# A hybrid decoder layer: the tokens' gate table moved from GpSimd to VectorE, and one transposed token tile copied out a weight piece earlier

## The chip, the cores and the metric

One NeuronCore of one Trainium2 chip. The engines are TensorE (PE in the profile, with its weight loads as PEld), VectorE (DVE), ScalarE (ACT), GpSimd (POOL) and SyncE (SP), which only issues transfers here. The metric is device time in microseconds (us). The time of the kernel before is 1771.23 us, the median of three runs from 1770.09 to 1771.25 us.

## What is computed

The reference is one layer on 512 tokens of 1024 channels: a mixer (gated delta rule and RG-LRU), a cross attention over 256 memory tokens, and a mixture of experts, then a last RMSNorm. The change touches the experts' part only:

```python
logits = xt @ w_router + b_router                 # 512 x 32
top_logit, top_e = lax.top_k(logits, TOP_K)       # 4 of 32 experts for each token
gate = jax.nn.softmax(top_logit, axis=-1)
...
gt = jnp.minimum(xblk @ w_gate[e] + b_gate[e], SWIGLU_LIMIT)
up = jnp.clip(xblk @ w_up[e] + b_up[e], -SWIGLU_LIMIT, SWIGLU_LIMIT)
hid = (up + 1.0) * (gt * jax.nn.sigmoid(SWIGLU_ALPHA * gt))
return hid @ w_down[e] + b_down[e]
...
y = yb.reshape(n_rows, D) * row_gate[:, None]
out = jax.ops.segment_sum(y, row_tok, num_segments=n_tok + 1)[:n_tok]
```

The tokens' rows are sorted by expert into blocks of 128 rows of one expert (`xblk`), and the blocks' results are summed up by token.

## The kernel before

All weights are float32. Each 128x1024 piece of a weight matrix is split in two parts: ScalarE writes the high part (`hi`, L1003 in the experts, L713 before them), VectorE subtracts it from the weights and writes the low part (`lo`, L1888 in the experts, L1616 before them), and TensorE multiplies three products of parts. In the experts a matrix has 8 pieces, a block of 128 rows needs 24 (gate 0 to 7, up 8 to 15, down 16 to 23), and there are 6 buffers of split pieces, so that ScalarE writes piece c when TensorE has used piece c-6. The 4 MB matrices lie in a ring of three; SyncE starts the load that reuses a place when VectorE has written the last low part out of it.

The order of the work is written out by hand on each engine, with semaphores between them. Each of the engines runs its list in order, so whatever stands behind a waiting instruction waits too.

**Around the router.** The last projection of the attention is done in 16 pieces, c = 0 to 15. TensorE's order is: piece 9, transposes of token tile 0, piece 10, transposes of tile 1, pieces 11 and 12, router products of tile 0 (L1411; they wait until the four copies of tiles 0 and 1 are out, `tr_evac`), piece 13, router of tile 1 and half the transposes of tiles 2 and 3, piece 14, halves of their router products, piece 15, the rest. VectorE at step c writes the low part of piece c+2, adds the residual at c = 7 and c = 11 (L1812), and copies the transposes out with `evac_h2` (L1883). ScalarE writes the high part of piece c+2 when TensorE has used piece c.

**Before and in the loop of the experts.** TensorE, VectorE and ScalarE do the first block as soon as the tables stand. POOL's list at that point is, with its lines: gather the rows of the second block (L583), build the gate table (L602 to L614), clear `gate_sb`, wait until the gates lie in DRAM (`gate_out`), two additions that make row numbers (`take`, L591), gather the rows' gates (L595), and then in the loop fetch the bias rows of the next block (L629), gather the rows of the block after it, and scatter the block's result. ScalarE waits for the gates of the rows before it scales a block's result (L1071); TensorE waits for the bias rows (`bias4_in`) before the first matmul of a block (L1496).

The gate table `g_parts` holds, for each token and each of 32 experts, the token's gate or zero, split in three parts. It is read once, in the last of the 32 blocks: TensorE transposes it (L1526, after `iota_ready` has reached 2), ScalarE copies it out (L1061), and the products with the experts' output biases (L1561) start the sum of the last rows. VectorE's list in a block (`expert_lo`) is: low parts 6 to 12, the product with the sigmoid (L2045), low parts 13 to 18, clipping and product of the two halves of the hidden rows (L2056, L2058, each twice), the low parts of the hidden rows (L2061) with pieces 19 to 21 between, then `x_lo` and pieces 22 and 23. After each half of the hidden rows TensorE transposes it (L1533) and goes on to the down matrix (L1546). The low parts 0 to 5 of the next block stand at the end of the loop's body.

Of the kernel before, what the change touches and what calls it, by code (L numbers as in the profile page):

```python
# [20 lines left out]
ALU = mybir.AluOpType  # L21
ACT = mybir.ActivationFunctionType
AX_X = mybir.AxisListType.X
F32 = mybir.dt.float32
BF16 = mybir.dt.bfloat16
F32R = mybir.dt.float32r
# [3 lines left out]
P = 128  # L30
# [4 lines left out]
def build_layer(nc, x, mem, norm_mix, w_in, dn_conv, dn_a_log, dn_dt_bias, dn_norm, rg_conv, rg_conv_b,  # L35
# [33 lines left out]
    with ExitStack() as ctx:  # L69
# [64 lines left out]
        def split_w(c, part):  # L134

            i = c % NSPLIT
            return wsp[:, (i + 2) % 4, part] if i < 4 else wsp_b[:, 5 - i, part]
# [216 lines left out]
        nf_row, bd_rows, bd_parts = ring[:, GM, 0, :], ring[:, GM, 1, :], split_w(0, 0)  # L354
        g_parts, g_stack = extra[:, 4, 0:NT * 3 * E].rearrange("p (t c) -> p t c", t=NT), bias4[0:3 * E, T:2 * T]
# [87 lines left out]
        def _(pool):  # L443
            chain = [0]

            def link(ins):
                chain[0] += 1
                ins.then_inc(pool_c, 1)
                pool.wait_ge(pool_c, chain[0])
# [97 lines left out]
            e_row = extra[:, 4, 384:384 + E]  # L547
# [54 lines left out]
            pool.wait_ge(codes_ready, 2)  # L602
            top_e = extra[:, 5, 128:160].rearrange("p (t k) -> p t k", t=NT)
            one = extra[:, 5, 256:512].rearrange("p (t k e) -> p t k e", t=2, k=TOPK)
            for t in range(0, NT, 2):
                for u in range(2):
                    for k in range(TOPK):
                        last = pool.tensor_scalar(one[:, u, k], e_row, top_e[:, t + u, k:k + 1], gates[:, t + u, k:k + 1], ALU.is_equal, ALU.mult)  # L608
                link(last)
                link(pool.tensor_tensor(one[:, :, 0:2], one[:, :, 0:2], one[:, :, 2:4], ALU.add))  # L610
                link(pool.tensor_tensor(g_parts[:, t:t + 2, 2 * E:3 * E], one[:, :, 0], one[:, :, 1], ALU.add))
            for c in range(2):
                link(pool.tensor_copy(g_parts[:, :, E * c:E * (c + 1)].bitcast(F32R), g_parts[:, :, 2 * E:3 * E]))
            pool.tensor_tensor(g_parts[:, :, 2 * E:3 * E], g_parts[:, :, 2 * E:3 * E], g_parts[:, :, 0:E], ALU.subtract).then_inc(iota_ready, 1)  # L614
# [970 lines left out]
        def _(dve):  # L1585
# [341 lines left out]
            for c in range(N_CO):  # L1927
# [11 lines left out]
                if c == 11:  # L1939
                    evac_h2(1, 0, 6, 3)  # L1940
                    evac_h2(1, 1, 7, 4)
# [96 lines left out]

            def expert_lo(n, last=False):
# [37 lines left out]

            expert_lo(n_more, last=True)
# [51 lines left out]
```

## Time and profile before

| what | value |
|---|---|
| median of three runs | 1771.23 us |
| the profiled execution's own time | 1772.93 us |
| its span in the trace | 1771.2 us |
| TensorE busy | 1690.2 us, 95% of the span |
| VectorE busy | 1437.0 us, 81% |
| ScalarE busy | 1274.6 us, 72% |
| GpSimd busy | 527.8 us, 30% |
| mean granted clock of TensorE | 0.987 of full speed |

The busy share of TensorE is so high that the view of busy times says little more than that time can be won only where TensorE stands still or runs at the lower of its two clock levels (1.2 instead of 2.4 GHz). The experts take the stretch from about 580 us to the end. The profile's queues and lines are read with the chain of waits (the work that ended last, followed back), the list of waits, and each engine's timeline; where a group of like instructions is merged, its duration runs from the first start to the last end. Starts are in us from the span's start.

### The profile page before, as it was taken

Reading aid. Unit: us, or ns where it says so; the run is one execution under the profiler, and the core shown is the slowest. Engines: PE = TensorE matmul, PEld = TensorE weight load, DVE = VectorE, ACT = ScalarE, POOL = GpSimd, SP = SyncE. Lnnn points to the kernel's source line nnn. Section 1 sums busy time; section 2 is a strip of 40 time slices with the busy share of each in tenths; the row PEclk is TensorE's granted clock in tenths of the full one; section 3 lists DMA queues with packets and bytes.
Section 4 is the critical chain, followed back from the end, with each engine's and each line's share of the span. In section 5 each row is a group of like instructions: output and inputs, shape, how many; then the busy total and the mean of one; then the engine's idle time right before and its main releaser. Section 6 shows DMA issues by size and latency. Waiting matters only on the chain.

```text
span 1771.2 us, 24520 instructions
## 1 busy us (share of the span) xinstructions
PE 1690.2 (95%) x8065; PEld 1385.7 (78%) x8065; DVE 1437.0 (81%) x1531; ACT 1274.6 (72%) x1452; POOL 527.8 (30%) x624
## 2 busy tenths in 40 slices
PE   6999799899899989999999999999999999999997
PEld 3778598787768768888888888888888888888885
DVE  3558686663347969999999999999999999999997
ACT  4453454464435668888888888888888888888885
POOL 3453552200022822242222222232232323232232
PEclk9999999999998989999999999999999999999999
DMA  7312100042014879999999999999999999999993
GB/s 249 119 51 100 41 1 1 24 190 95 26 82 191 330 271 369 360 383 378 355 371 371 382 359 370 360 382 379 351 371 369 379 364 369 360 380 379 353 371 120
DMA packets 53880, 476.18 MB, mean 269 GB/s; under 512 B 10503, under 2 KB 11640, under 8 KB 29266
## 3 DMA queue, kind: packets, MB, share of 16 engines
q1 hardware_dynamic: 42528, 450.70, 62.8%
q0 software_dynamic: 11120, 24.91, 6.3%
q8 instruction: 25, 0.41, 0.1%
q14 instruction: 13, 0.11, 0.0%
q10 hardware_dynamic: 194, 0.06, 0.0%
HBM read 461.24 MB, written 23.08 MB: 273 GB/s over the span
## 4 chain that ended last, share of the span: by engine, by line
PE 61%; DVE 18%; issue 12%; ACT 6%; POOL 3%; DMA 1%; ACTq 0%; POOLq 0%; DVEq 0%
PE ps L1546 20%; PE ps L1506 17%; PE ps L1143 10%; PE ps L1304 4%; DVE wsp L1888 4%; DVE extra L2058 2%; DVE extra L2056 2%; DVE wsp_b L1888 2%; ACT extra L1048 2%; POOL extra L608 1%; PE ps L1533 1%; PE ps L1227 1%; DVE wf L1616 1%; PE ps L1239 1%; PE ps L1496 1%
## 5 line engine op out<-in xcount | busy, mean ns | idle before, releaser
L1888 DVE TENSOR_TENSOR wsp<-ring,wsp 128x1024 fp32r<-128x1024 f32 x512 | 601.1, 1219 | 26.6 <-ACT wsp L1003 26.1
L1003 ACT ACTIVATE wsp<-ring 128x1024 fp32r<-128x1024 f32 x388 | 387.0, 1051 | 80.2 <-PE ps L1488 53.0
L580 POOL TENSOR_TENSOR guard<-guard 1x1 f32<-1x1 f32 x219 | 133.8, 616 | 763.0 <-ACT extra L1071 327.9
L1506 PE MATMUL ps<-wsp,x_hi 128*128 128x512 f32 x1152 | 311.8, 392 | 0.6 <-DVE x_lo L2014 0.6
L1888 DVE TENSOR_TENSOR wsp_b<-ring,wsp_b 128x1024 fp32r<-128x1024 f32 x256 | 301.8, 1218 | 9.8 <-ACT wsp_b L1081 9.1
L1506 PEld LDWEIGHTS ps<-wsp,x_hi 128*128 128x128 f32 x1152 | 217.5, 189 | 50.1 <-issue 1.1
L1003 ACT ACTIVATE wsp_b<-ring 128x1024 fp32r<-128x1024 f32 x194 | 205.5, 1060 | 32.3 <-PE ps L1506 11.0
L1506 PE MATMUL ps<-wsp,x_lo 128*128 128x512 f32 x576 | 179.1, 392 | 0.0
L1616 DVE TENSOR_TENSOR wf<-ring,wf 128x1024 fp32r<-128x1024 f32 x64 | 81.3, 1273 | 111.8 <-ACT wf L713 111.8
L713 ACT ACTIVATE wf<-ring 128x1024 fp32r<-128x1024 f32 x80 | 84.2, 1055 | 117.4 <-PE ps L1143 62.2
L1143 PE MATMUL ps<-act_hi,wf 128*128 128x512 f32 x512 | 161.6, 397 | 2.6 <-DVE wf L1616 2.1
L1081 ACT ACTIVATE wsp<-ring 128x1024 fp32r<-128x1024 f32 x124 | 131.9, 1064 | 36.8 <-PE ps L1546 36.8
L1546 PE MATMUL ps<-wsp_b,hid_hi 128*128 128x512 f32 x512 | 140.2, 395 | 0.0
L1506 PE MATMUL ps<-wsp_b,x_hi 128*128 128x512 f32 x512 | 136.8, 389 | 0.0
L1546 PE MATMUL ps<-wsp,hid_hi 128*128 128x512 f32 x512 | 136.8, 389 | 0.0
L1506 PEld LDWEIGHTS ps<-wsp,x_lo 128*128 128x128 f32 x576 | 108.6, 189 | 23.4
L1488 PE MATMUL ps<-wsp,x_hi 128*128 128x512 f32 x384 | 118.2, 389 | 0.0
L1143 PEld LDWEIGHTS ps<-act_hi,wf 128*128 128x128 f32 x512 | 95.7, 188 | 27.5 <-issue 8.1
L1546 PEld LDWEIGHTS ps<-wsp,hid_hi 128*128 128x128 f32 x512 | 96.1, 188 | 20.0
L1506 PEld LDWEIGHTS ps<-wsp_b,x_hi 128*128 128x128 f32 x512 | 96.1, 188 | 20.0
L1546 PEld LDWEIGHTS ps<-wsp_b,hid_hi 128*128 128x128 f32 x512 | 93.6, 188 | 22.8 <-issue 4.8
L1143 PE MATMUL ps<-act_lo,wf 128*128 128x512 f32 x256 | 99.8, 390 | 0.0
(380 smaller groups left out, 2993.9 us busy)
## 6 DMA issues: line engine op xcount, KB each, us to landing
ring<-in_w_gate_dram SPq DMA_DIRECT2D x32, 4096.0 KB, 15.3
ring<-in_w_up_dram SPq DMA_DIRECT2D x32, 4096.0 KB, 14.4
ring<-in_w_down_dram SPq DMA_DIRECT2D x32, 4096.0 KB
ring<-in_w_in_dram SPq DMA_DIRECT2D x6, 2048.0 KB, 12.0
ring<-in_w_ckv_dram SPq DMA_DIRECT2D x4, 2048.0 KB, 10.1
ring<-in_w_out_dram SPq DMA_DIRECT2D x2, 2048.0 KB, 10.6
ring<-in_w_cq_dram SPq DMA_DIRECT2D x2, 2048.0 KB, 11.1
ring<-in_w_co_dram SPq DMA_DIRECT2D x2, 2048.0 KB, 10.6
```

The lines of the kernel that those rows point to most:

```text
L580: return pool.tensor_tensor(guard[:, i:i + 1], guard[:, 0:1], guard[:, 0:1], ALU.mult)
L713: act.activation(parts_of(f, 0), piece(f), ACT.Copy).then_inc(wfh_ready, 1)
L1003: act.activation(split_w(c, 0), ring[:, m, k], ACT.Copy).then_inc(hi_ready, 1)
L1048: act.activation(gs, ps[:, 0:2, :].rearrange("p b f -> p (b f)"), ACT.Sigmoid, scale=1.702).then_inc(sg_ready, 1)
L1081: act.activation(split_w(c, 0), ring[:, GM, c], ACT.Copy).then_inc(hi_ready, 1)
L1143: last = pe.matmul(o, parts_of(f, w)[:, k], a[:, k], start=(k == 0 and w == 0 and a is a_hi), stop=(k == KT - 1 and a is a_lo))
L1304: last = pe.matmul(ps[:, banks[b]], a[:, rows + kk, ts], parts_of(f, w)[:, kk], start=(first and kk == 0 and a is a_hi and w == 0), stop=( ...
L1488: o = pe.matmul(ps[:, bank + i], xp[:, c % KT * P:(c % KT + 1) * P], split_w(c, w)[:, i * 512:(i + 1) * 512], start=False, stop=(last_k an ...
L1506: last = pe.matmul(ps[:, 2 * j + i], xp[:, k * P:(k + 1) * P], split_w(c, part)[:, i * 512:(i + 1) * 512], start=False, stop=(k == KT - 1 ...
L1546: last = pe.matmul(ps[:, 4 + i], xp[:, k * P:(k + 1) * P], split_w(c, part)[:, i * 512:(i + 1) * 512], start=(k == 0 and xp is hid_hi and ...
L1616: dve.tensor_tensor(parts_of(f, 1), piece(f), parts_of(f, 0), ALU.subtract).then_inc(wfl_ready, 1)
L1888: dve.tensor_tensor(split_w(c, 1), ring[:, (GM + c // KT) % 3, c % KT], split_w(c, 0), ALU.subtract).then_inc(lo_ready, 1)
```

## The change

Two edits. First, the gate table is built by VectorE at the start of the last block, ahead of its `expert_lo`, and no longer by POOL between its first gather and the clearing of `gate_sb`. On POOL one table took 16 products of 128x32, 4 additions, 2 copies and a subtraction; on VectorE it takes, for each pair of token tiles, two comparisons, two products and two reductions, each over 128x128, and after both pairs two copies and a subtraction, with a wait after each group. The definition of `e_row` moves up for this. Second, the two copies of token tile 1's transposes stand at c = 10 and not at c = 11.

```diff
--- before.py
+++ after.py
@@ -352,6 +352,7 @@
         LAST_BANKS = ((0, 1), (2, 3), (6, 7), (4, 5))
         last_tok, last_f, last_oh = extra[:, 5, :].bitcast(I32), extra[:, 5, :], bias4[:, 0:T]
         nf_row, bd_rows, bd_parts = ring[:, GM, 0, :], ring[:, GM, 1, :], split_w(0, 0)
+        e_row = extra[:, 4, 384:384 + E]
         g_parts, g_stack = extra[:, 4, 0:NT * 3 * E].rearrange("p (t c) -> p t c", t=NT), bias4[0:3 * E, T:2 * T]
         ylo_ready, YLO = yt_ready, 4
         sum_mm, SUM_MM = out_mm, 8
@@ -544,7 +545,6 @@
             link(pool.iota(it_i[:, 417:418], pattern=[[0, 1]], base=4 * T + 1, channel_multiplier=4))
             link(pool.tensor_copy(ef[:, 64:80], it_i[:, 64:80]))
             link(pool.tensor_copy(ef[:, 288:418], it_i[:, 288:418]))
-            e_row = extra[:, 4, 384:384 + E]
             link(pool.tensor_copy(ef[:, 0:E], it_i[:, 0:E]))
             link(pool.tensor_copy(e_row, it_i[:, 0:E]))
             link(pool.tensor_scalar(ef[:, 32:64], ef[:, 0:E], float(CAP * P), None, ALU.mult))
@@ -599,19 +599,6 @@
 
             link(take(0, tok_tab, slice(CAP, CAP + 1)))
             gather()
-            pool.wait_ge(codes_ready, 2)
-            top_e = extra[:, 5, 128:160].rearrange("p (t k) -> p t k", t=NT)
-            one = extra[:, 5, 256:512].rearrange("p (t k e) -> p t k e", t=2, k=TOPK)
-            for t in range(0, NT, 2):
-                for u in range(2):
-                    for k in range(TOPK):
-                        last = pool.tensor_scalar(one[:, u, k], e_row, top_e[:, t + u, k:k + 1], gates[:, t + u, k:k + 1], ALU.is_equal, ALU.mult)
-                link(last)
-                link(pool.tensor_tensor(one[:, :, 0:2], one[:, :, 0:2], one[:, :, 2:4], ALU.add))
-                link(pool.tensor_tensor(g_parts[:, t:t + 2, 2 * E:3 * E], one[:, :, 0], one[:, :, 1], ALU.add))
-            for c in range(2):
-                link(pool.tensor_copy(g_parts[:, :, E * c:E * (c + 1)].bitcast(F32R), g_parts[:, :, 2 * E:3 * E]))
-            pool.tensor_tensor(g_parts[:, :, 2 * E:3 * E], g_parts[:, :, 2 * E:3 * E], g_parts[:, :, 0:E], ALU.subtract).then_inc(iota_ready, 1)
             link(pool.memset(gate_sb[:], 0.0))
             pool.wait_ge(gate_out, 16)
             pool.wait_ge(acc_in, 16 * NT)
@@ -1936,7 +1923,7 @@
                 if c == 9:
                     evac_h2(0, 0, 4, 1)
                     evac_h2(0, 1, 5, 2)
-                if c == 11:
+                if c == 10:
                     evac_h2(1, 0, 6, 3)
                     evac_h2(1, 1, 7, 4)
                 if c == 13:
@@ -2036,6 +2023,25 @@
             dve.wait_ge(codes_ready, 1)
             n_more = dve.value_load(nblocks[0:1, 1:2], min_val=E - 1, max_val=MAXB - 4)
 
+            def gate_table():
+
+                one = extra[:, 5, 256:512].rearrange("p (t k e) -> p t k e", t=2, k=TOPK)
+                for t in range(0, NT, 2):
+                    for u in range(2):
+                        ins = dve.tensor_tensor(one[:, u], e_row.unsqueeze(1).to_broadcast([P, TOPK, E]),
+                                                tf4[:, t + u].unsqueeze(2).to_broadcast([P, TOPK, E]), ALU.is_equal)
+                    link(ins)
+                    for u in range(2):
+                        ins = dve.tensor_tensor(one[:, u], one[:, u], gates[:, t + u].unsqueeze(2).to_broadcast([P, TOPK, E]), ALU.mult)
+                    link(ins)
+                    for u in range(2):
+                        ins = dve.tensor_reduce(g_parts[:, t + u, 2 * E:3 * E], one[:, u].rearrange("p k e -> p e k"), AX_X, ALU.add)
+                    link(ins)
+                for c in range(2):
+                    ins = dve.tensor_copy(g_parts[:, :, E * c:E * (c + 1)].bitcast(F32R), g_parts[:, :, 2 * E:3 * E])
+                link(ins)
+                dve.tensor_tensor(g_parts[:, :, 2 * E:3 * E], g_parts[:, :, 2 * E:3 * E], g_parts[:, :, 0:E], ALU.subtract).then_inc(iota_ready, 1)
+
             def expert_lo(n, last=False):
 
                 for c in range(NSPLIT, 13):
@@ -2075,6 +2081,7 @@
                 for c in range(NSPLIT):
                     lo(c, n * SPLIT + (SPLIT + c + 1))
 
+            gate_table()
             expert_lo(n_more, last=True)
             dve.wait_ge(bias_split, 4)
             dve.tensor_tensor(bd_parts[E:2 * E], bd_rows[E:2 * E], bd_parts[E:2 * E], ALU.subtract).then_inc(bias_split, 1)
```

## Rows read from the trace of the kernel before

**Rows 1.** the page, its first line

```profile
span 1771.2 us, 24520 instructions
```

**Rows 2.** waits from 575 to 660 us: engine, line, waited for: total us, times, longest

```profile
PE ps L1496 <- DMA bias<-bias_parts: 10.5, 1, 10.5
```

**Rows 3.** chain of waits from 540 to 660 us: start, us, what

```profile
585.42 17.81 POOL extra L608 x8
...
616.98 1.30 POOL extra L614
...
623.37 4.22 DMA bias<-bias_parts
```

**Rows 4.** PE timeline in the first block: start, us, group

```profile
605.26 0.75 PE L1533 MATMUL ps<-ident,extra 128*128 128x128 f32 x4 [0.16 <-DVE extra L2058]
```

**Rows 5.** chain of waits, the same transposes one block and thirty blocks later

```profile
655.00 0.75 PE ps L1533 x4
...
1705.78 0.75 PE ps L1533 x4
```

**Rows 6.** one full block length, busy us: PE, PEld, DVE, ACT, POOL; clock, DMA share, GB/s

```profile
678.20:714.50 36.30, 36.15 (x166) 29.75 (x165) 33.71 (x34) 31.28 (x33) 8.76 (x14) 1.00 0.94 369
```

**Rows 7.** DMA of the gate rows (L419): issue, and us to landing

```profile
L419 SPq DMA_DIRECT2D gate_rows<-gates x1: 370/370/370, 584.7 to 584.7; - x1
...
DMA to landing us min/median/max: 9.9/9.9/9.9
```

**Rows 8.** line L608, POOL: ns min/median/max, first and last start

```profile
L608 POOL TENSOR_SCALAR extra<-extra,gates x16: 462/474/8689, 585.4 to 611.3; 128x32 f32<-128x32 f32 x16
```

**Rows 9.** DVE timeline in the first block: where PSUM is read after the pieces

```profile
602.43 0.68 DVE L2056 TENSOR_SCALAR extra<-ps 128x512 f32<-128x512 f32 x1
```

**Rows 10.** PE timeline around the router: start, us, group, idle before

```profile
531.95 1.03 PE L1404 MATMUL ps<-ident,resid 128*128 128x128 f32 x8
...
540.62 2.77 PE L1411 MATMUL ps<-w_rt,chan 128*128 128x32 f32 x16 [2.18 <-DVE chan L1883]
```

**Rows 11.** chain of waits after it, 540 to 660 us

```profile
543.39 5.20 PE ps L1304 x12
548.59 1.71 PE ps L1411 x16
...
551.20 2.77 PE ps L1304 x12
```

**Rows 12.** DVE timeline around the router

```profile
533.52 1.21 DVE L1616 TENSOR_TENSOR wf<-ring,wf 128x1024 fp32r<-128x1024 f32 x1
...
536.85 1.23 DVE L1616 TENSOR_TENSOR wf<-ring,wf 128x1024 fp32r<-128x1024 f32 x1 [2.04 <-ACT wf L713]
...
539.19 1.28 DVE L1883 COPY chan<-ps 128x512 f32<-128x512 f32 x2
```

**Rows 13.** one microsecond at the router, one after the boundary (columns as in rows 6)

```profile
547.00:548.00 1.00, 1.00 (x3) 0.75 (x3) 0.00 (x0) 0.00 (x0) 0.00 (x0) 0.50 0.00 0
629.00:630.00 1.00, 1.00 (x4) 0.73 (x3) 0.41 (x1) 0.98 (x2) 0.57 (x2) 0.50 0.22 90
```

**Rows 14.** DVE timeline, the choice of experts

```profile
563.00 0.49 DVE L1920 TENSOR_TENSOR extra<-extra 128x128 f32<-128x128 f32 x2
563.52 0.69 DVE L1924 TENSOR_REDUCE extra<-extra 128x32 f32<-128x128 f32 x2
```

**Rows 15.** DVE timeline before and in the last block

```profile
1714.42 4.63 DVE L1888 TENSOR_TENSOR wsp<-ring,wsp 128x1024 fp32r<-128x1024 f32 x4
...
1721.23 4.78 DVE L1888 TENSOR_TENSOR wsp<-ring,wsp 128x1024 fp32r<-128x1024 f32 x4
...
1738.71 0.68 DVE L2056 TENSOR_SCALAR extra<-ps 128x512 f32<-128x512 f32 x1
1739.43 1.14 DVE L2058 SCALAR_TENSOR_TENSOR extra<-extra 128x512 f32<-128x512 f32 x1
```

**Rows 16.** PE timeline in the last block

```profile
1742.23 0.75 PE L1533 MATMUL ps<-ident,extra 128*128 128x128 f32 x4 [0.80 <-DVE extra L2058]
```

## The prediction

> **What bounds the kernel now.** I read the page first: a span of 1771.2 us [rows 1], in which TensorE is nearly always busy. So time can come only from the places where it stands still or runs at its lower clock. I looked for them in three steps: the waits and the chain of waits of the stretch where the changed code runs; the engines' timelines there; and a block length from the middle of the loop, to know what an undisturbed block looks like. That last row [rows 6] shows TensorE busy 36.15 of 36.3 us at full clock, VectorE 33.71, and the DMA engines at 0.94: TensorE sets the pace, VectorE and the weight stream have some 7% and 6% left.
>
> Both edits touch a place where TensorE stands still. At the first block boundary it waits 10.5 us for the bias rows [rows 2]. The chain goes back through POOL to the gate table [rows 3]: the table starts at 585.42 us with its products, and the bias transfer, which stands behind it on POOL, is issued only just before 623.37 and lands at 627.6. TensorE was ready 10.5 us before, at 617.1 to 617.2. At the router it waits 2.18 us for VectorE's copy of tile 1 [rows 10].
>
> **The boundary.** The same transposes start at 605.26 in block 0 [rows 4], at 655.00 in block 1 and at 1705.78 in block 30 [rows 5]. An undisturbed block is (1705.78 - 655.00) / 29 = 36.23 us; the first boundary made its block 49.74 us long, so the disturbance costs 13.5 us. Of these 10.5 are the wait, and the other 3.0 the lower clock after it, granted at 0.50 [rows 13]. What must be ready instead, with the table gone from POOL? The additions of row numbers wait for the gates in DRAM, a transfer issued at 584.7 that landed 9.9 us later [rows 7], at 594.6. Then come two additions, the gather of gates, and the bias rows. POOL can be held up by VectorE here: the first product of the table took 8.689 us where its like take 0.47 [rows 8], while VectorE ran low parts without a break. So I take the late bound: the additions get through only when VectorE turns to PSUM at 602.43 [rows 9]. Before, from the end of the table (616.98 + 1.30 = 618.3) to the bias transfer (623.4) POOL needed 5.1 us for these steps, the gather among them, and the transfer landed 4.2 us on [rows 3]. From 602.4 that gives 611.7, and 605 if POOL isn't held up. With the slow landing of 9.9 us [rows 7] in place of 4.2 it is 617.4 at the latest, against a need at 617.2. So I take the whole 13.5 us, and for the bound one wait of up to 1 us, or some 3 us if several of these go long together. The gates are issued before the bias rows and are wanted no sooner. TensorE finds the rest as at any boundary: low parts and `x_lo` come from lists that the edit doesn't touch. The weight stream has to deliver 13.5 us of work sooner, but only the same matrices in the same rhythm as in the blocks behind it, at 0.94 [rows 6].
>
> The Trainium skill (SBUF — State Buffer, "Who interferes with whom") says that a VectorE instruction with two SBUF inputs and a GpSimd instruction that reads SBUF exclude each other for a whole instruction, the later one waiting. The row of 8.689 us agrees. By that rule the additions, which read SBUF, are the ones held up, and the sum would be that of my late bound, again 13.5 us; a POOL that is never held up gives the same.
>
> **The router.** TensorE waits from 538.44 to 540.62 for the copies of tile 1 [rows 10], which VectorE does from 539.19, behind the low part of piece 13 and two residual additions [rows 12]. The transposes that they read were over at 532.98 [rows 10]. At c = 10 they follow the low part that ran from 533.52 to 534.73, so with 1.28 us they end at about 536.1, in the gap of 2.04 us before 536.85 in which VectorE waited for ScalarE [rows 12]. They cost VectorE nothing, delay no low part, and are ready 2.3 us before TensorE asks. It loses no 2.18 us then. After the wait the granted clock was half [rows 13], and that goes too if the pause caused it: the router products took 2.77 us where the next ones take 1.71 (1.06), and piece 13 took 5.20 where the next piece takes 2.77 (2.43) [rows 10, 11]. Sum 2.18 + 1.06 + 2.43 = 5.7 us. If the clock fell for another reason it is 2.2 us. Next in line is piece 14's low part: ScalarE can start its high part at 538.44, and at about 1.2 us for each part it is there near 541, while TensorE asks for it after 1.7 + 2.8 + 1.7 us of router and piece 13, at 544.6 or later. Then come the logits, which follow TensorE's own products in the same distance as before. The residual addition that ends this stretch waits for TensorE's last piece, so the gain goes on to the tables.
>
> **The last block.** The table is new work on VectorE at 1721.23 [rows 15]. The nearest rows are the choice of experts, of the same shapes: two comparisons 0.49 us, two reductions 0.69 [rows 14]. I take the products at the comparisons' price. So 2 x (0.49 + 0.49 + 0.69) = 3.34; the two copies at no more than 0.49, the subtraction 0.25; seven waits at 0.02 to 0.03 as between the two rows of [rows 14], 0.15 in all. Together 4.2 us, with bounds of 3.7 (copies at nothing) and 5.0 (POOL's pending reads slip in between and hold it up).
>
> What hides it? From 1721.23 to 1738.71 are 17.48 us, with 13 low parts and one product of their size. At the pace of four in 4.63 us, about 1.137 us each [rows 15], they need 15.9. So 1.6 us of room is there and 4.2 - 1.6 = 2.6 us reach L2056. Behind it TensorE already waits 0.80 us for the second half of the hidden rows [rows 16], so this delay goes into its time in full. A part may come back: the first L2058 takes 1.14 us where L2056 of the same shape takes 0.68 [rows 15], and POOL is at work then; later it may not be. I take 2.5, with ends of 2.1 and 3.4. TensorE's first piece of the last stretch of buffers may come up to half a us late; it waits for the hidden rows anyway, so this isn't added. POOL's wait for `iota_ready` 2 at the end, and TensorE's, are met long before (the table ends near 1725.5).
>
> The definition of `e_row` that moves up costs nothing: it issues no instruction. The sum: 13.5 + 5.7 - 2.5 = 16.7 us off a span of 1771.2, that is 1754.5. The profiled execution itself took 1772.93, the median is 1771.23 and equals the span, so I take 1754.5 as the median too.
>
> **The rivals.**
>
> - **The clock falls in the last block.** TensorE will stand for some 1.6 us ahead of the first half of the hidden rows and 0.8 ahead of the second. At the router a pause of 2.18 us was followed by half clock [rows 10, 13]; after the 0.80 us of this block [rows 16] I found no fall. If it falls, work of 3 to 7 us at half clock loses 1.7 to 3.4 us: 1756 to 1758. Chance 0.17. The Trainium skill (TensorE: Matmul & The Clock Gate, "What's actually happening") has the low level as the default state, which activity lifts; by that a pause more broken up than the router's may or may not do, and the sum would be 1756 to 1758 or unchanged.
> - **The boundary keeps a wait.** POOL's small transfers land late among the weights (9.9 against 4.2 us are both in the rows), and a wait of 1 to 5 us stays, with a fall of the clock: 1756 to 1761. For it speaks that POOL was held up for 8.7 us at once; against it, a margin of 5 us with the landing that was seen for the bias. Chance 0.09.
> - **The copies don't free the router.** The wait moves to the low part of piece 13 or 14, or the clock is low anyway: 3.5 to 5.7 us less gain, 1758 to 1760. The rows give each of them its margin. Chance 0.05.
> - **The weight stream takes the 13.5 us back,** because it used the pause to get ahead: 1768. But the place in the ring, not the rate, starts each load, and later blocks run at TensorE's pace. Chance 0.02.
> - **Slower than before:** POOL enters the loop at another phase against VectorE and is held up in every block, so that a gather is late each time. Each of some 30 blocks would have to lose over 16.7 / 30 = 0.56 us before the kernel is slower, as at 1 us a block: 1784. Against it: POOL's phase in the loop is set by TensorE's and ScalarE's signals, and full blocks show 0.15 us of idle TensorE in 36.3 [rows 6]. Chance 0.01.
>
> **How the numbers follow.** The forecast as it stands has 0.66: 1753.6 to 1755.7 from the bounds of the last block, and with a median that moves by a us between measurements 1753.0 to 1756. The first rival and the near part of the second take the high end to 1758; above it lie 0.1, and below 1753 less. All cases but the last lie faster than 1771.2 by more than 0.2% (3.5 us), which is about what a measurement of this kernel can tell from no change; the fourth by 3.2 us is within it.
>
> **What would show it.** Right: no wait of TensorE for the bias rows, and L1533 of block 1 starts 36.2 us after that of block 0; L1411 after piece 12 without a wait and at full clock, the experts 5.7 us sooner; the bias rows' transfer issued near 600 to 606; VectorE's table 4.2 us long, L2056 of the last block 2.6 us later against its block's start, and 2.4 us of waiting before the two groups of L1533. Wrong: a wait for `bias` or `gate_sb` left at the boundary; half clock after 1725 or in piece 13; blocks longer than 36.24 us; a table of 6 us or more.

## The result, and the profile after

The changed kernel takes 1757.47 us (median of four, 1755.71 to 1759.12) against 1770.66 us. The ratio is 0.9928, with a 95% interval of 0.9916 to 0.9940: 12.7 us less, between 10.6 and 14.9. The forecast was 1754.5, with 1753.0 to 1756 for its main case and a high end of 1758 that takes in the first rival. The measured median lies in the rival's part of that range, 3.0 us above the forecast. The profiled execution of the changed kernel is the longest of its four, so its rows stand 1.7 us above the median. Line numbers above the change in the file stay; those from POOL's removed block to VectorE's new function are 13 lower, those behind it in `expert_lo` 6 higher and behind its last call 7 higher, so that L1506 is L1493, L1888 is L1875, L1533 is L1520 and L2056 is L2062.

The page, its first line and the one of busy times:

```profile
span 1757.5 us, 24512 instructions
...
PE 1687.4 (96%) x8065; PEld 1383.2 (79%) x8065; DVE 1438.7 (82%) x1546; ACT 1274.6 (73%) x1452; POOL 499.5 (28%) x601
```

**The router.** The chain of waits (start, us, what), to be read beside [rows 10, 11], and VectorE's timeline, beside [rows 12]:

```profile
534.47 5.46 PE ps L1291 x24
539.93 1.70 PE ps L1398 x16
541.63 2.85 PE ps L1291 x12
```

```profile
535.01 1.21 DVE L1603 TENSOR_TENSOR wf<-ring,wf 128x1024 fp32r<-128x1024 f32 x1
...
536.21 1.26 DVE L1870 COPY chan<-ps 128x512 f32<-128x512 f32 x2
538.34 1.23 DVE L1603 TENSOR_TENSOR wf<-ring,wf 128x1024 fp32r<-128x1024 f32 x1 [0.86 <-ACT wf L700]
```

The copies (L1870) now run in VectorE's gap. Pieces 11 and 12 (24 products), the router products and piece 13 follow each other with nothing between, where 2.18 us of waiting stood; the router products take 1.70 us instead of 2.77, the piece 2.85 instead of 5.20.

**The boundary.** POOL's timeline, then the chain of waits:

```profile
580.61 0.11 POOL L602 MEMSET gate_sb<- 128x1 f32 x1
591.30 1.93 POOL L591 TENSOR_TENSOR idx<-tabs 128x1 int32<-128x1 int32 x2 [10.59 <-issue]
594.01 1.22 POOL L595 DMA_INDIRECT gate_sb<-gate_rows,idx  x1 [0.78 <-POOL idx L591]
...
596.59 0.58 POOL L616 DMA_DIRECT2D bias<-bias_parts  x1
```

```profile
600.51 0.75 PE ps L1520 x4
601.26 11.16 PE ps L1533 x48
612.42 0.48 PE ps L1483 x2
...
636.76 0.75 PE ps L1520 x4
```

POOL clears `gate_sb` at once, waits 10.59 us for the gates' transfer, and fetches the bias rows (L616) at 596.59, 15.8 us before TensorE multiplies by them at 612.42. TensorE goes from the down matrix to the bias products with no pause. The transposes of blocks 0 and 1 are 36.25 us apart, where it was 49.74.

**The last block.** VectorE's timeline, beside [rows 14, 15]:

```profile
1703.36 0.49 DVE L2031 TENSOR_TENSOR extra<-extra 128x128 f32<-128x128 f32 x2
...
1704.42 0.70 DVE L2038 TENSOR_REDUCE extra<-extra 128x32 f32<-128x128 f32 x2
...
1706.94 0.36 DVE L2041 CAST extra<-extra 128x128 fp32r<-128x128 f32 x2
1707.34 0.29 DVE L2043 TENSOR_TENSOR extra<-extra 128x128 f32<-128x128 f32 x1
1707.55 4.62 DVE L1875 TENSOR_TENSOR wsp<-ring,wsp 128x1024 fp32r<-128x1024 f32 x4
...
1723.44 0.69 DVE L2062 TENSOR_SCALAR extra<-ps 128x512 f32<-128x512 f32 x1
...
1725.48 1.15 DVE L2064 SCALAR_TENSOR_TENSOR extra<-extra 128x512 f32<-128x512 f32 x1
```

The table runs from 1703.36, and the low parts go on at 1707.55, so it takes 4.2 us. From there to L2062 it is 15.9 us, as forecast for 14 pieces without a gap, and from the table's start 20.08 us, against the 17.48 before: VectorE is 2.6 us late, as forecast. TensorE's timeline, and one row of five microseconds with the busy time of each engine and then the granted clock:

```profile
1708.82 1.20 PE L1493 MATMUL ps<-wsp,x_hi 128*128 128x512 f32 x4 [0.31 <-DVE wsp L1875]
...
1724.90 0.74 PE L1520 MATMUL ps<-ident,extra 128*128 128x128 f32 x4 [1.16 <-DVE extra L2064]
1726.69 0.91 PE L1520 MATMUL ps<-ident,extra 128*128 128x128 f32 x4 [1.04 <-DVE extra L2064]
1727.25 2.05 PE L1533 MATMUL ps<-wsp_b,hid_hi 128*128 128x512 f32 x4
```

```profile
1725.00:1730.00 5.00, 3.96 (x15) 3.19 (x16) 4.97 (x6) 1.68 (x3) 3.30 (x5) 0.71 0.00 0
```

TensorE waits 0.31 us for low part 6, then 1.16 and 1.04 us for the two halves of the hidden rows. From the transposes of block 1 to the last ones it is 1726.69 - 636.76 = 1089.9 us, before 1742.23 - 655.00 = 1087.2: the table costs 2.7 us. Behind the two waits the clock is low in part of the stretch (0.71 on average): four products take 2.05 us. From there to the end of the span it is 30.8 us, before 29.0.

**How the two profiled executions add up.** The router products start at 539.77 in the changed one. In the one before they could have started at 538.44, where the wait began, so the changed one is 1.3 us late there; no edit touches the stages before. From there to the first bias products it takes 575.17 - 539.77 = 35.4 us against 579.82 - 538.44 = 41.4, 6.0 less (the pause, the clock, and 0.3 of other). From there to block 1's transposes it is 61.6 against 75.2 us, 13.6 less. The last block gives back 2.7, and the stretch behind it 1.8. The sum is 1.3 - 6.0 - 13.6 + 2.7 + 1.8 = -13.8 us, and the spans differ by 1771.2 - 1757.5 = 13.7.

### The profile page after: what moved, and what is told of

It is laid out like the page before. It is cut to its first block, busy times and chain, and to the rows that moved or that the text cites. A ratio compares the mean times of both kernels' runs of the same rounds, so it can differ in the third digit from the quotient of the medians.

```text
span 1757.5 us, 24512 instructions
## 1 busy us (share of the span) xinstructions
PE 1687.4 (96%) x8065; PEld 1383.2 (79%) x8065; DVE 1438.7 (82%) x1546; ACT 1274.6 (73%) x1452; POOL 499.5 (28%) x601
## 4 chain that ended last, share of the span: by engine, by line
PE 61%; DVE 19%; issue 13%; ACT 6%; POOL 1%; DMA 0%; ACTq 0%; DVEq 0%; POOLq 0%
PE ps L1533 20%; PE ps L1493 17%; PE ps L1130 10%; DVE wsp L1875 5%; PE ps L1291 4%; DVE extra L2064 2%; DVE extra L2062 2%; DVE wsp_b L1875 2%; ACT extra L1035 2%; PE ps L1520 1%; PE ps L1214 1%; PE ps L1226 1%; DVE wf L1603 1%; PE ps L1382 1%; PE ps L1483 1%
## 5 line engine op out<-in xcount | busy, mean ns | idle before, releaser
L1875 DVE TENSOR_TENSOR wsp<-ring,wsp 128x1024 fp32r<-128x1024 f32 x512 | 600.7, 1219 | 24.0 <-ACT wsp L990 24.0
L580 POOL TENSOR_TENSOR guard<-guard 1x1 f32<-1x1 f32 x219 | 129.9, 599 | 772.5 <-ACT extra L1058 337.5
L1493 PE MATMUL ps<-wsp,x_hi 128*128 128x512 f32 x1152 | 310.3, 391 | 0.8 <-DVE x_lo L2001 0.5
L1875 DVE TENSOR_TENSOR wsp_b<-ring,wsp_b 128x1024 fp32r<-128x1024 f32 x256 | 301.3, 1218 | 0.1
L1493 PEld LDWEIGHTS ps<-wsp,x_hi 128*128 128x128 f32 x1152 | 216.1, 188 | 50.2 <-issue 0.9
L1493 PE MATMUL ps<-wsp,x_lo 128*128 128x512 f32 x576 | 178.3, 391 | 0.0
L1533 PE MATMUL ps<-wsp_b,hid_hi 128*128 128x512 f32 x512 | 141.8, 399 | 0.0
L1493 PE MATMUL ps<-wsp_b,x_hi 128*128 128x512 f32 x512 | 136.8, 389 | 0.0
L1533 PE MATMUL ps<-wsp,hid_hi 128*128 128x512 f32 x512 | 136.8, 389 | 0.0
L1493 PEld LDWEIGHTS ps<-wsp,x_lo 128*128 128x128 f32 x576 | 108.1, 188 | 23.2
L1533 PEld LDWEIGHTS ps<-wsp_b,hid_hi 128*128 128x128 f32 x512 | 94.5, 190 | 23.1 <-issue 4.7
L1533 PEld LDWEIGHTS ps<-wsp,hid_hi 128*128 128x128 f32 x512 | 96.1, 188 | 19.9
L1493 PEld LDWEIGHTS ps<-wsp_b,x_hi 128*128 128x128 f32 x512 | 96.1, 188 | 19.9
## 6 DMA issues: line engine op xcount, KB each, us to landing
ring<-in_w_out_dram SPq DMA_DIRECT2D x2, 2048.0 KB, 10.6
ring<-in_w_co_dram SPq DMA_DIRECT2D x2, 2048.0 KB, 10.5
```

The costliest lines, as they stand in the source:

```text
L580: return pool.tensor_tensor(guard[:, i:i + 1], guard[:, 0:1], guard[:, 0:1], ALU.mult)
L1493: last = pe.matmul(ps[:, 2 * j + i], xp[:, k * P:(k + 1) * P], split_w(c, part)[:, i * 512:(i + 1) * 512], start=False, stop=(k == KT - 1 ...
L1533: last = pe.matmul(ps[:, 4 + i], xp[:, k * P:(k + 1) * P], split_w(c, part)[:, i * 512:(i + 1) * 512], start=(k == 0 and xp is hid_hi and ...
L1875: dve.tensor_tensor(split_w(c, 1), ring[:, (GM + c // KT) % 3, c % KT], split_w(c, 0), ALU.subtract).then_inc(lo_ready, 1)
```

## The experiments

Each time stands against runs of the kernel before on the same chip. A saving is worked out from the ratio and that median. The changed kernel's own times come from the first comparison only, so "under the changed kernel" below is a difference of two medians from different comparisons. The medians of the kernel before in the three comparisons are 1770.66, 1771.66 and 1770.74 us, so such a difference is uncertain by about a us from this alone. A table at the end of this part compares the profiled executions over the stretch that holds the last block.

### One edit at a time

The table alone on VectorE:

```diff
-                if c == 10:
+                if c == 11:
                     evac_h2(1, 0, 6, 3)
```

> The first edit alone: the gate table goes from GpSimd to VectorE, tile 1's copies stay at c = 11. My theory (the two edits are independent; the boundary gives back 13.5 us, the table costs some 2.7 us on VectorE and 1.5 us of half clock after it): 9 to 11 us under the kernel before, TensorE still waiting 2.2 us at the router. Rival (the edits share a gain, or the router's 5.6 us are mostly lost again behind it): this kernel alone is within 2 us of the changed one, that is some 12 to 13 us under before.

Measured: 1761.02 us, ratio 0.9942 (0.9928 to 0.9956), 10.3 us less. It is what the boundary and the last block should give together. The rival's 12 to 13 us lie at or beyond the end of the interval, which is 7.8 to 12.8 us. TensorE's row at the router shows the pause and the slow products as before:

```profile
541.07 2.73 PE L1398 MATMUL ps<-w_rt,chan 128*128 128x32 f32 x16 [2.18 <-DVE chan L1870]
```

The copies alone, the kernel before with

```diff
-                if c == 11:
+                if c == 10:
                     evac_h2(1, 0, 6, 3)
```

> The second edit alone: only the copies of tile 1's transposes move to c = 10. My theory: no wait of TensorE before the router products and no half clock in piece 13, 5 to 6 us under before at the tables, and since the boundary's chain runs through GpSimd from the tables on, the whole of it reaches the end. Rival 1 (the low clock has another cause): 2.2 us. Rival 2 (the gain is eaten behind the router): under 1 us.

Measured: 1767.17 us, ratio 0.9972 (0.9962 to 0.9981), 5.0 us less. The interval is 3.4 to 6.7 us, so both theories that had the router's gain small fall. In the profile the router products start without a wait and take 1.86 us. The wait at the boundary is all there, in the list of waits:

```profile
PE ps L1496 <- DMA bias<-bias_parts: 10.0, 1, 10.0
```

The two savings add to 15.3 us, against 12.7 for both edits, with intervals of 10.6 to 14.9 for the latter and some 3 us to each side for the former. They overlap; the rival that the edits share a gain isn't borne out, and the difference is taken up below.

### What the table costs where it stands

First the changed kernel with no table built, so its last sum has wrong biases; it only gives a price:

```diff
-            gate_table()
+            dve.memset(g_parts[:, 0, 0:1], 0.0).then_inc(iota_ready, 1)
             expert_lo(n_more, last=True)
```

> The changed kernel without a gate table: VectorE clears one column and signals, so the output biases of the last sum are not what they should be. It prices the table on VectorE in the last block. My theory: TensorE's two waits ahead of the hidden rows' transposes shrink from 1.16 and 1.04 us to one of some 0.5, no half clock behind them, and the time is 3.5 to 4.5 us under the changed kernel (2.7 for VectorE, 1.5 for the clock). Rival (the table hides in VectorE's spare time): within 1 us of the changed kernel.

Measured: 1753.59 us, ratio 0.9899 (0.9884 to 0.9914), 17.9 us less than before and 3.9 us under the median of the changed kernel, inside what was expected. The difference of the two savings, 17.9 and 12.7, is 5.2 us, so the 3.9 is a price to about a us at best. The rival, that the table hides in spare time, falls. TensorE waits once, 1.02 us, and its products run at full speed behind it:

```profile
1722.47 0.75 PE L1520 MATMUL ps<-ident,extra 128*128 128x128 f32 x4 [1.02 <-DVE extra L2064]
1722.98 1.17 PE L1533 MATMUL ps<-wsp_b,hid_hi 128*128 128x512 f32 x4
```

Then the table in two parts. VectorE does tiles 0 and 1 where it did the whole, and the rest after its last low part:

```diff
-            gate_table()
+            gate_table(0, 2)
             expert_lo(n_more, last=True)
             dve.wait_ge(bias_split, 4)
             dve.tensor_tensor(bd_parts[E:2 * E], bd_rows[E:2 * E], bd_parts[E:2 * E], ALU.subtract).then_inc(bias_split, 1)
+            gate_table(2, NT)
```

TensorE transposes the table before the last piece of the down matrix, ScalarE copies it out behind the bias rows, the table has a semaphore of its own, and the token numbers of the last sum move to a place that the table doesn't use, so POOL needn't wait.

> The changed kernel with the table in two parts: tiles 0 and 1 (1.75 us) at the head of the last block, where VectorE had some 1.6 us of room; tiles 2 and 3, the copies and the subtraction (2.4 us) behind the last low part and the bias part, where VectorE waits for ScalarE; TensorE transposes the table before the last piece of the down matrix. My theory (the cost is VectorE's delay of the hidden rows, not the work itself): TensorE waits 0.8 to 1.0 us for the hidden rows as before, no half clock, and the time is 3 to 4 us under the changed kernel, within 1 us of the kernel without a table. Rival (the table's work costs wherever it stands, since the end of the block waits for it): no better than the changed kernel.

Measured: 1756.45 us, ratio 0.9913 (0.9898 to 0.9928). That is 1.0 us under the changed kernel, not 3 to 4: my number failed. The firmer comparison is with the kernel without a table, measured on the same chip beside it: 2.9 us more, where I had expected 1 at most. The hidden rows' wait was down to 0.78 us, but TensorE met the second part of the table:

```profile
1724.36 0.75 PE L1514 MATMUL ps<-ident,extra 128*128 128x128 f32 x4 [0.78 <-DVE extra L2065]
...
1736.13 0.64 PE L1523 MATMUL ps<-ident,extra 128*96 128x128 f32 x4 [1.24 <-DVE extra L2044]
```

A wait of 1.24 us and 0.4 us of transposes stand where there was nothing. So the table was moved again, from the same frame. The work on tiles 0 and 1 stays at the head of the last block:

```diff
             def expert_lo(n, last=False):
...
+                if last:
+                    table_is(2)
                 for i in range(2):
                     dve.wait_ge(hidhi_ready, n * 2 + (i + 1))
...
             expert_lo(n_more, last=True)
+            table_sum(2)
+            table_parts()
             dve.wait_ge(bias_split, 4)
```

> The split table, moved further into VectorE's idle places: tiles 0 and 1 at the head of the last block, the comparisons of tiles 2 and 3 in the 0.69 us in which VectorE waits for ScalarE after the hidden rows, their products, sums and parts (1.8 us) right behind the last low part, the bias part after them. My theory (what was left of the table's cost in the split kernel was TensorE's wait of 1.24 us for the second part): that wait is gone, the transposes of 0.4 us stay, and the time is 1 to 2 us under the split kernel, so 2 to 3 us under the changed one. Rival (the split kernel's rest is the order of ScalarE and TensorE at the end, not VectorE): no better than the split kernel.

Measured: 1753.38 us, ratio 0.9904 (0.9890 to 0.9918), 17.0 us less than before and 3.1 us under the split kernel (1.6 by the two savings), near what the kernel without a table takes. The rival, no better than the split kernel, is not borne out: over the last stretch the profile is 1.8 us shorter (table below). VectorE ends the table at 1731.71, TensorE takes it at 1732.52 without a wait; before the hidden rows it waits 0.78 us, as before the change:

```profile
1729.80 0.48 DVE L2035 TENSOR_TENSOR extra<-extra,gates 128x128 f32<-128x128 f32 x2
...
1731.42 0.29 DVE L2045 TENSOR_TENSOR extra<-extra 128x128 f32<-128x128 f32 x1
```

```profile
1722.15 0.75 PE L1514 MATMUL ps<-ident,extra 128*128 128x128 f32 x4 [0.78 <-DVE extra L2066]
...
1732.52 0.60 PE L1523 MATMUL ps<-ident,extra 128*96 128x128 f32 x4
```

The split kernel and this one differ only in the order of VectorE's list. So it isn't the work that costs, but its place there: more than the room holds ahead of the hidden rows, or its second part behind the moment at which TensorE wants it.

### How late POOL may come at the boundary

Here POOL makes tiles 0 and 1 of the table where it made all, VectorE tiles 2 and 3 at the head of the last block and the parts in its idle time after the hidden rows. The cut is shown against the kernel before, whose block of POOL code it halves:

```diff
             gather()
             pool.wait_ge(codes_ready, 2)
...
-            for t in range(0, NT, 2):
-                for u in range(2):
+            for u in range(2):
...
+            pool.tensor_tensor(g_parts[:, 0:2, 2 * E:3 * E], one[:, :, 0], one[:, :, 1], ALU.add).then_inc(iota_ready, 1)
             link(pool.memset(gate_sb[:], 0.0))
```

> The table shared: GpSimd builds tiles 0 and 1 where it built the whole before, ahead of the first block boundary; VectorE does tiles 2 and 3 at the head of the last block and the parts in its idle 0.69 us. It tests the margin at the boundary. Half the table took GpSimd 19 us (585.4 to 604.5); from some 580.6 it ends near 600, the bias rows are fetched near 604 and land at 608 to 614, against a need at 612.4. My theory (GpSimd may come that late): at most 1 us of wait for the bias rows, the time within 1 us of the kernel without a table plus 0.5. Rival (the small transfers land late): a wait of 1 to 5 us and half clock behind it, so no better than the changed kernel.

Measured: 1753.21 us, ratio 0.9903 (0.9886 to 0.9919), 17.2 us less than before, level with the last kernel. POOL's timeline, then TensorE's:

```profile
578.49 17.80 POOL L607 TENSOR_SCALAR extra<-extra,gates 128x32 f32<-128x32 f32 x8
596.38 0.85 POOL L609 TENSOR_TENSOR extra<-extra 128x128 f32<-128x128 f32 x1
...
601.41 0.59 POOL L625 DMA_DIRECT2D bias<-bias_parts  x1 [0.44 <-issue]
```

```profile
609.60 0.62 PE L1541 MATMUL ps<-wsp_b,hid_lo 128*128 128x512 f32 x2
610.06 0.64 PE L1491 MATMUL ps<-bias,sel 128*128 128x512 f32 x2
```

The bias rows are fetched at 601.41 and TensorE multiplies by them at 610.06, with no wait: 8.7 us suffice in this execution. In the changed kernel it is 15.8 us. The rival of late small transfers isn't borne out at this boundary: there is no wait in the profile, and the four times lie within 1.1 us.

### What the pauses cost, and what the clock costs

The kernel before with matmuls into a free bank during the router's pause:

```diff
                         pe.wait_ge(iota_ready, 1)
+                        pe.wait_ge(tr_evac, 2 * (2 * NT + MT) + 2)
+                        fill_wait(14, 4)
                         router(0, 0, 4)
```

> The kernel before, with 14 matmuls of 256 columns into a free bank in the router's pause (they should last some 2 us; nothing reads them). It separates the pause from the clock. My theory (the half clock behind the pause follows from TensorE standing still): the pause stays filled, the clock stays full, and the time is 3 to 3.5 us under before. Rival (the clock falls there for another reason, the pause alone is the loss): within 1 us of before, with half clock in piece 13 as before.

Measured: 1768.18 us, ratio 0.9990 (0.9981 to 0.9999), 1.8 us less, with 0.2 to 3.4 as its interval. TensorE's timeline:

```profile
536.94 1.83 PE L1120 MATMUL ps<-sel 128*128 128x256 f32 x14
539.18 1.97 PE L1411 MATMUL ps<-w_rt,chan 128*128 128x32 f32 x16 [0.40 <-DVE chan L1885]
540.99 0.70 PE L1304 MATMUL ps<-wf,act_hi 128*128 128x512 f32 x2
```

The pause lasts as long as before, filled but for 0.40 us, and behind it the router products take 1.97 us, not 2.77, and the clock stays full. But the median says 1.8 us, which fits neither theory's number, and not the 3.5 that the first profile shows. Its 12 times lie between 1766.4 and 1769.1; the 17 of the kernel before on that chip lie between 1767.3 and 1773.7, and seven of them are below 1768.7. Further profiles of both kernels follow below.

The same in the changed kernel's last block:

```diff
                 for b in range(2):
+                    if last_block:
+                        fill_wait((8, 7)[b], 7)
                     pe.wait_ge(hid_ready, n * 2 + (b + 1))
```

> The changed kernel, with 8 and 7 such matmuls ahead of the two groups of transposes of the last block's hidden rows, where TensorE waits 1.16 and 1.04 us. Same question at the other place: if the half clock behind those waits is a regular part of the change's price, the time is about 1.5 us under the changed kernel and the first products of the down matrix run at full clock; if the fall of the profiled execution was one of chance, within 0.5 us of it. The matmuls may themselves delay the transposes by up to 0.3 us.

Measured: 1755.74 us, ratio 0.9915 (0.9901 to 0.9929), 1.7 us under the changed kernel's median. From the last transposes to the end it is 1754.4 - 1725.20 = 29.2 us, against 30.8. The difference of the medians can't tell the two theories apart, since the intervals of the two ratios overlap; the further profiles below show the fall in some executions of the changed kernel and not in others.

The kernel before, and the changed one, profiled twice more each, unchanged:

> The kernel before, unchanged, profiled once more. Its times spread from 1767.3 to 1774.9 us, more than those of its variants. My theory: whether the clock falls behind the router's pause of 2.2 us differs from execution to execution; where it doesn't fall, the router products take 1.9 us and piece 13 takes 2.8, and the time is some 3.5 us less. Rival: the fall behind the router is there each time and the spread comes from other places.

> As the look before this one: the kernel before, profiled a third time, for the same two theories.

> The changed kernel, unchanged, profiled once more. My theory: the fall behind the two waits of the last block is one of chance too; without it the down matrix runs at full clock from its first products and the span is some 1.5 us less than 1757.5. Rival: it is there each time.

> As the look before this one: the changed kernel, profiled a third time, for the same two theories.

TensorE at the router in the two further profiles of the kernel before (spans 1771.8 and 1766.2 us):

```profile
541.51 3.36 PE L1411 MATMUL ps<-w_rt,chan 128*128 128x32 f32 x16 [2.18 <-DVE chan L1883]
```

```profile
540.04 1.94 PE L1411 MATMUL ps<-w_rt,chan 128*128 128x32 f32 x16 [2.18 <-DVE chan L1883]
```

and in the last block of the first further profile of the changed kernel (span 1753.6 us):

```profile
1722.62 0.75 PE L1520 MATMUL ps<-ident,extra 128*128 128x128 f32 x4 [1.20 <-DVE extra L2064]
1724.41 0.75 PE L1520 MATMUL ps<-ident,extra 128*128 128x128 f32 x4 [1.04 <-DVE extra L2064]
1724.91 1.17 PE L1533 MATMUL ps<-wsp_b,hid_hi 128*128 128x512 f32 x4
```

The waits are the same to a few hundredths, 2.18 us here and 1.20 and 1.04 there. The clock is not. It fell behind the router's pause in three of four profiles that have the pause (the kernel before in two of three, and the one with the table alone). Behind the last block's waits it fell in two of three profiles of the changed kernel, and not in the one with the table alone, where the end came 29.2 us after the last transposes. From the router's start to the first bias products it is 39.2 us with the fall (579.82 - 540.62) and 35.7 without (575.73 - 540.04): 3.5 us. From the last transposes to the end it is 30.8 and 30.6 us with it, 29.2 without: 1.5 us.

The rival, that the spread comes from other places, is right in part too. The two further profiles of the kernel before differ by 5.6 us: 3.0 from the router's start to the first bias products, 1.5 before the router, 0.7 from there to block 1's transposes, 0.4 behind them. Two more places show in the profiles.

One lies ahead of all edits. TensorE stands for 1.67 to 1.72 us near 58 to 60 us in each of the 14 profiles, for a low part. The clock falls behind it in four of them (the changed kernel's first, the copies alone, the split table, the kernel before once) and stays full in ten. The stretch from 60 to 75 us, in the first profile of the changed kernel and in the first further one (busy time of each engine, then the granted clock):

```profile
60.00:75.00 15.00, 14.98 (x57) 11.90 (x58) 9.91 (x13) 7.79 (x13) 6.27 (x4) 0.89 0.00 1
```

```profile
60.00:75.00 15.00, 14.72 (x63) 11.84 (x64) 11.44 (x16) 8.52 (x13) 7.78 (x5) 1.00 0.02 3
```

Of the nine profiles without a pause at the router, the three with this fall start the router products at 539.6 to 540.1 us, the six without it at 537.3 to 538.0.

The other is the first boundary. In the five profiles with the whole table on POOL TensorE waits 9.9 to 10.5 us there, and the block's transposes follow the last ones after 49.74, 49.70 and 48.83 us (the kernel before), 49.12 (the copies alone) and 48.04 (the filled pause). With 36.24 for an undisturbed block the boundary costs 11.8 to 13.5 us, and 1.7 of the 6.6 us by which the filled pause's profile is shorter than the first one of the kernel before are gained there.

From block 1's transposes to the end of the span, which leaves out the router, the boundary and all ahead of them:

| kernel | us |
|---|---|
| before, five profiles with the table on POOL | 1116.2 to 1116.6 |
| changed, clock falls in the last block (two) | 1120.7, 1120.5 |
| changed, clock stays full | 1119.1 |
| table alone, clock stays full | 1118.8 |
| changed, waits filled with matmuls | 1119.1 |
| no table | 1116.8 |
| table in two parts | 1118.7 |
| second part in the idle places | 1116.9 |
| shared with GpSimd | 1117.2 |

The table at the head of the last block costs 1.9 to 2.3 us against none where the clock stays full, and 3.7 to 3.9 where it falls.

## Where the prediction held and where not, point by point

The mechanism was right at all three places, but for the clock in the last block, which only the first rival had. The main case, 1753.0 to 1756 with 0.66, was missed: the median of 1757.47 lies in the range because its high end made room for the first rival. The saving of 16.7 us that was forecast lies outside the measured 10.6 to 14.9. Each of the terms was read off one execution, and in that one the clock was low behind the router's pause and long behind the boundary's. The median holds executions in which it isn't.

**The boundary, 13.5 us: held in the profiled execution, at the high end of five.** The first two traces give 13.6, the five profiles with the table on POOL 11.8 to 13.5, 12.8 on average, and all three parts of the argument came out: the additions of row numbers waited for the gates, POOL was held up no longer than I had allowed, the bias rows were there long before. The first of the two additions started at 591.30 and both were done at 593.23; the late bound of 602.4, which is 597.6 in this execution (L2062), was too careful by 4.4 us. The pair took 1.93 us, where it takes 0.32 at other places. I think that VectorE left POOL in between two of its low parts there, which I had not looked for in the rows before; no experiment was made on it. (The prediction's 605 for a POOL that isn't held up should be 603.9 by its own numbers; nothing rests on it.)

**The router, 5.7 us: right in the profiled execution, too high as a term of the median.** The pause of 2.18 us is in every execution. The 3.5 us of low clock are in most of them only. I took the sum from one execution and set it against the median, with the remark that the span equals it. The prediction had bounds for the last block but none for this term. The medians of the kernel before lie between an execution with the fall and one without. The edit alone gave 5.0 us, and the filled pause 1.8.

**The last block, 2.5 us: held for VectorE, the clock came on top.** The table took 4.2 us, and 2.7 reached TensorE. The two copies took 0.36 us where I had allowed 0.49. The part that might have come back didn't: the last L2064 took 1.15 us. POOL ran a cast beside it (from 1725.48), as it did beside the slow L2058 before (from 1739.41); that this is what slows it was not tested. The two waits of TensorE together are 2.2 us, where I had forecast 2.4. The rival with the falling clock, given 0.17 and 1.7 to 3.4 us, is what two of four profiled executions with these waits show, at 1.5 us. Half clock after 1725 was one of the signs that I had named for being wrong, and it came. 0.17 was too low a chance, and the price was a little too high. The kernel without a table puts both at 3.9 us by the medians. The bounds of 2.1 to 3.4 us for this block give 1754.1 to 1755.4, not the 1753.6 to 1755.7 of the prediction; the measured time lies above either.

**The sum.** The last block is 2.7 us, and 1.5 more in about half of the executions, 3.5 in all; the medians say 3.9. With that, 5.0 for the router and 12.8 for the boundary, the forecast would have been 12.8 + 5.0 - 3.9 = 13.9 us. Measured are 12.7, with 10.6 to 14.9 as the interval, so nothing is left that these runs could resolve. The clock behind the pause at 60 us adds some 2 us to an execution or not, by the two groups of router starts above, and no edit touches that stretch. It fell in the changed kernel's first profile and not in that of the kernel before, and that goes with the 1.3 us that the changed one was late at the router. With four times of each kernel, chance of this kind alone can move the medians' difference; its share was not separated.

**The rivals behind.** No transfer of weights took back what the pause had given; blocks stay at 36.24 us, (1724.41 - 634.47 - 2.7) / 30. No wait of POOL showed up in each block. The wait did not move to piece 13 or 14.

## What to carry to other kernels

A chain that passes through a slow list on a helper engine can be cut by taking one piece of work out of it, but the piece has to go where its new engine is idle, not just where it is off the old chain: the same table cost 3.9 us at the head of the last block, and nothing that the times could tell when only half of it, which is what the room there holds, stayed at the head and the rest came up to 28 us later, or was shared with the old engine. Before work is moved to an engine, count its room up to the next thing that somebody waits for (here 1.6 us for 4.2 of work), and cut the work to that size. A pause of TensorE of 2 us cost more than itself here, but only in part of the executions. Take such a term from several profiles, and every other term too, and look at the spread of the times of the kernel before.

## What the runs showed of the hardware

After the same pause of 2.18 us TensorE's clock fell in three profiles and stayed full in one, and after waits of 1.16 to 1.20 and 1.04 us it fell in two of three profiles of the changed kernel and not in that of the table alone. After a pause of 1.67 to 1.72 us near 60 us it fell in four of 14. 1.83 us of matmuls in the pause, and 0.40 us left of it, went with full clock in the one profile taken.

POOL's instruction that starts the gather of gates took 7.76 us in the last block of the changed kernel, where VectorE ran low parts without a break from 1716.63 to 1723.5; nobody waited for it. It took 7.76 us in all five profiles with the whole table at the head of that block. POOL's timeline:

```profile
1716.69 7.76 POOL L595 DMA_INDIRECT gate_sb<-gate_rows,idx  x1 [0.53 <-issue]
1724.48 0.41 POOL L580 TENSOR_TENSOR guard<-guard 1x1 f32<-1x1 f32 x1
```

At the boundary it took 1.22 us from 594.01, and there VectorE ran low parts without a break as well, from 590.84 to 597.7; in the blocks between it never took over 2.1 us in this profile:

```profile
590.84 3.49 DVE L1875 TENSOR_TENSOR wsp<-ring,wsp 128x1024 fp32r<-128x1024 f32 x3
594.24 2.35 DVE L1875 TENSOR_TENSOR wsp_b<-ring,wsp_b 128x1024 fp32r<-128x1024 f32 x2
```

The Trainium skill (SBUF — State Buffer, "Who interferes with whom") infers that a subtraction of two SBUF inputs on VectorE doesn't hold up the making of descriptors on GpSimd. The 31 short instructions don't speak against it, the long one may. A gather also reads its row numbers from SBUF, and no run here separates that reading from the writing of descriptors, so what held up the one instruction stays open.
